# Attention in a hybrid decoder layer: the diagonal matrix of negated row maxima moves from one VectorE product to eight scaled ScalarE copies

## The chip, the cores and the metric

The kernel runs on one core of a Trainium2 chip, in one launch. The metric is device time in microseconds, the median of repeated runs; a profile of one more execution stands beside them. The engines are TensorE (PE in the rows), VectorE (DVE), ScalarE (ACT), GpSimd (POOL) and SyncE (SP), which issues the DMA transfers. Each engine works through its own list of instructions in order and meets the others through semaphores.

## The reference, cut to what matters

One decoder layer over 2048 positions with model width 1024. The part that matters here is the pair of attentions, each with 8 query heads of width 64: a sparse one (A) over selected keys, and a sliding-window one (B) over 128 keys with a learned sink per head.

```
# B, for each block of 128 queries
logits = q @ k.T * scale + bias;  masked to the window
m = max(max(logits, axis=-1), sink)
e = exp(logits - m)
p = e / (sum(e) + exp(sink - m))
o = p @ v
# A is a plain softmax over the selected keys: exp(logits - max) / sum, then @ v
```

So both need a row maximum per query and head, and both subtract it before the exponential.

## The kernel before, in words

The kernel has four stages one after the other: `front` (input projection, scores and selection), `attend`, `merge` (gates, output projection, layer norm) and `ffn`. The change is in `attend`, which takes about 775 to 1655 us of the profiled span.

`attend` works on 32 blocks b = 0 to 31: for each of the 16 tiles of 128 queries first kind 0 (attention A, with n+1 key tiles), then kind 1 (attention B, with two key tiles). Block b is `(kind, n) = (b % 2, b // 2)`. The logits are formed twice. The first time (`top`) they are laid out with queries on the partitions, in the two PSUM halves `sq`, and VectorE takes their maxima: kind 0 with the fused add and maximum on L951 into `mx`, kind 1 with a reduction on L940 into `mm8`. Then `negmax` finishes `mm8` [128 queries x 8 heads] (L960 for kind 0, L958 for kind 1) and builds `dg`, 128 x 1024: for each head the 128 x 128 matrix with the negated maximum on its diagonal, as the product of `nid` (the negated identity) and `mm8` on L963 (the statement begins on L963 and ends on L966). TensorE multiplies ones by `dg` (`spread`, L1141, two halves) and so has the negated maxima along the free axis in every row; ScalarE copies them into `q2` (L897), from where they come into the second set of logits as part of a matmul. In that second set (`logits`, L1097 to L1103, PSUM tile `stp`) keys are on the partitions. ScalarE takes the exponential (L868) and its rounded copy `phi` (L870), GpSimd the remainder `plo` (L810), and TensorE multiplies both with the values (`values`, L1122 to L1124) into `ov`. ScalarE and VectorE each empty half of `ov` after the last pair of a block (`finish`, L879 and L880 on ScalarE, L976 and L977 on VectorE).

The order on every engine comes from one list `plan`, made by a small planner in ticks: a tick has one `logits`, one `values` in two halves three steps behind, and in between up to five pieces of the next blocks' preparation (`q`, `kv`, `vt`, `top`, `max`, `spread`). Each engine walks the same list and does its own part of each entry. On ScalarE, `q` is two copies of the loaded queries (L842, L843), which VectorE then completes on L984; `kv` is two copies (L850, L851); `vt` two (L858, L859); `logits` is L868 and L870. Before the change, ScalarE does nothing at `max`, and goes past it. `max` stands right before the next block's `q` in most blocks, or before a `finish`, and `spread` comes one tick later.

These waits matter here. TensorE's `spread` waits for `dgd`, the finished `dg`. Its `logits` of a block wait for `q2d`, both halves of `q2`; a `top` that reuses a half of `sq` waits until what was in it is read; the first `values` of a block wait for `eva` and `evd`, the emptied `ov` of the block before.

Of the kernel before, what the change touches and what calls it, by code (L numbers as in the profile page):

```python
# [20 lines left out]
ALU = mybir.AluOpType  # L21
ACT = mybir.ActivationFunctionType
AX = mybir.AxisListType
# [5 lines left out]
P = 128  # L29
# [3 lines left out]
HEADS = 8  # L33
# [12 lines left out]
CH = 512  # L46
# [527 lines left out]
def stage_attend(nc, zt, mask, bands, sinks, yt, ident):  # L574

    with Stage(nc, "att") as s:
# [26 lines left out]
        nid = s.sb("nid", [P, P], F32)  # L603
        irep = s.sb("irep", [P, CH], BF16)
        ones = s.sb("ones", [P, P], F32R)
        dg = s.sb("dg", [P, QW], F32R)
# [3 lines left out]
        mx = s.sb("mx", [P, HEADS, NCH], F32)  # L610
        mm8 = s.sb("mm8", [P, HEADS], F32)
        snk = s.sb("snk", [P, HEADS], F32)
        early = ExitStack()

        def initial(name, shape):
# [12 lines left out]
        stp = s.ps("stp", [P, 2, QW])  # L628
        ov = s.ps("ov", [P, QW])
        banks = stp[:].rearrange("p a b -> p (a b)")  # L630
        names = ("lka", "lva", "lba", "lbq", "lsn", "rnd", "kdone", "tp", "tpe", "vdone", "bhd", "bld", "bqd", "c0", "c1", "c2", "cst",
                 "lq0", "lq1", "lm0", "lm1", "lm2", "lb0", "lb1", "qr", "qd", "kh", "kd", "vt", "vh", "vd", "sqd", "sqr", "dvl",
                 "dgd", "nm", "q2d", "std", "ex", "ph", "pl", "pv", "eva", "evd", "rc", "yd", "st0", "st1")
        S = {n: s.sem(n) for n in names}
# [16 lines left out]
        while nv < len(steps):  # L651
            room, left = [], 2.2
            while pend and left > 0.3 and len(room) < 5:
                op, b, x = pend[0]
# [34 lines left out]
            if go:  # L689
                b, i = steps[nv]  # L690
# [126 lines left out]
        @block.scalar  # L817
        def _(act):
            def round_bias(kind):
                act.wait_ge(S["lbq"], 16 * (kind + 1))  # L820
                act.activation(bq[:, kind], bqa[:], ACT.Copy).then_inc(S["bqd"], 1)

            def round_near(kind):
                act.wait_ge(S["lba"], 32 * (kind + 1))
                if kind:
                    act.wait_ge(S["rnd"], 2)
                act.activation(bhi[:, kind], ba[:], ACT.Copy).then_inc(S["bhd"], 1)

            act.wait_ge(S["lka"], 32)
            act.activation(khh[:], ka[:], ACT.Copy).then_inc(S["rnd"], 1)  # L830
            round_bias(0)
            for t in range(2):
                act.wait_ge(S["tp"], t + 1)
                act.activation(vhi[:, 8 * t:8 * t + 8, 0:DH], banks[:, t * CH:(t + 1) * CH].rearrange("p (n c) -> p n c", n=8),
                               ACT.Copy).then_inc(S["tpe"], 1)
            round_near(0)

            def queries(b):
                act.wait_ge(S[f"lq{b % 2}"], 32 * (b // 2 + 1))
                if b >= NQ:  # L840
                    act.wait_ge(S["std"], first[b - NQ + 1])
                act.activation(qst[:, b % NQ, :], kr[:, b % 2, :], ACT.Copy, scale=SCALE).then_inc(S["qr"], 1)  # L842
                act.activation(q2[0:DH, b % NQ, :], kr[0:DH, b % 2, :], ACT.Copy, scale=SCALE).then_inc(S["qr"], 1)  # L843

            def window_keys(n):
                act.wait_ge(S[f"lb{n % 2}"], 96 * (n // 2 + 1))
                act.wait_ge(S["c0"], 3)
                if n >= 2:
                    act.wait_ge(S["std"], first[index[1, n - 2] + 1])
                act.activation(khb[:, n % 2], kbr[:, n % 2, 0], ACT.Copy)  # L850
                act.activation(khb[:, 2 + n % 3], kbr[:, n % 2, 1], ACT.Copy).then_inc(S["kh"], 1)  # L851

            def window_values(n):
                act.wait_ge(S["vt"], n + 1)
                if n >= 2:
                    act.wait_ge(S["pv"], first[index[1, n - 2] + 1])
                src = sq[:, where[("vt", index[1, n], 0)] % 2, 0:2 * P].rearrange("p (v g d) -> p v g d", v=2, g=2)
                act.activation(vhb[:, n % 2, :, 0:DH], src[:, 0], ACT.Copy)  # L858
                act.activation(vhb[:, 2 + n % 3, :, 0:DH], src[:, 1], ACT.Copy).then_inc(S["vh"], 1)  # L859

            def exponential(k):
                act.wait_ge(S["std"], k + 1)
                if k == 0:
                    act.wait_ge(S["bld"], 2)
                    act.wait_ge(S["bqd"], 2)
                if k >= PS:
                    act.wait_ge(S["pv"], k - PS + 1)
                act.activation(pf[:, k % PS, :], stp[:, k % 2, :], ACT.Exp).then_inc(S["ex"], 1)  # L868
                act.wait_ge(S["ex"], k + 1)
                act.activation(phi[:, k % PS, :], pf[:, k % PS, :], ACT.Copy).then_inc(S["ph"], 1)  # L870

            def evict(b):
                act.wait_ge(S["pv"], first[b + 1])
                if b >= 2:
                    act.wait_ge(S[f"st{b % 2}"], 16 * (b // 2))
                oe = ov[:, 0:CH].rearrange("p (a e q) -> p a e q", a=2, e=2)
                for e in range(2):
                    rows = slice(e * DH, (e + 1) * DH)
                    act.activation(den[rows, b % 2, 0:2], oe[DH:P, :, e, :], ACT.Copy)  # L879
                    last = act.activation(y[rows, b % 2, 0:2], oe[0:DH, :, e, :], ACT.Copy)  # L880
                last.then_inc(S["eva"], 1)

            for op, b, x in plan:
                if op == "q":
                    queries(b)
                    if b == 1:
                        round_bias(1)
                        round_near(1)
                elif op == "kv":
                    window_keys(seq[b][1])  # L890
                elif op == "vt":
                    window_values(seq[b][1])
                elif op == "logits":
                    exponential(first[b] + x)
                elif op == "spread":
                    act.wait_ge(S["nm"], 2 * b + x + 1)
                    act.activation(q2[DH:P, b % NQ, x * CH:(x + 1) * CH], sq[DH:P, where[(op, b, x)] % 2, :], ACT.Copy).then_inc(S["q2d"], 1)  # L897
                elif op == "finish":
                    evict(b)

        @block.vector
        def _(dve):
            links = 0

            def link(ins):
                nonlocal links
                links += 1
                ins.then_inc(S["dvl"], 1)
                dve.wait_ge(S["dvl"], links)
# [22 lines left out]
            def top(b, x):  # L932
                kind, n = seq[b]
                h, c = x
                i = top_no[("top", b, x)]
                k = where[("top", b, x)] % 2
                dve.wait_ge(S["sqd"], i + 1)
                if kind:
                    w = P * min(2, n + 1)
                    dve.tensor_reduce(mm8[:, h:h + 2], sq[:, k, :].rearrange("p (a b) -> p a b", a=2)[:, :, 0:w],  # L940
                                      AX.X, ALU.max).then_inc(S["sqr"], 1)
                    return
                w = min(CH, (n + 1) * P - c * CH)
                if n >= 2:
                    dve.wait_ge(S[f"lm{n % 3}"], 16 * ((n - 2) // 3 + 1))
                    m = msk[:, n % 3, c * CH:c * CH + w]
                else:
                    m = cm[:, P - n * P:2 * P]
                if i >= 2:
                    dve.wait_ge(S["sqr"], i - 1)  # L950
                dve.tensor_tensor_reduce(junk[:, i % 2, 0:w], sq[:, k, 0:w], m, 1.0, 4 * NEG, ALU.add, ALU.max,  # L951
                                         mx[:, h, c:c + 1]).then_inc(S["sqr"], 1)

            def negmax(b):
                kind, n = seq[b]
                dve.wait_ge(S["sqr"], top_end[b])
                if kind:
                    link(dve.tensor_tensor(mm8[:], mm8[:], snk[:], ALU.max))  # L958
                else:
                    link(dve.tensor_reduce(mm8[:], mx[:, :, 0:-(-(n + 1) * P // CH)], AX.X, ALU.max))  # L960
                if b:
                    dve.wait_ge(S["nm"], 2 * b)
                dve.tensor_tensor(dg[:].rearrange("p (h q) -> p h q", h=HEADS),  # L963
                                  nid[:].rearrange("p (o q) -> p o q", o=1).broadcast_to([P, HEADS, P]),
                                  mm8[:].rearrange("p (h o) -> p h o", o=1).broadcast_to([P, HEADS, P]),
                                  ALU.mult).then_inc(S["dgd"], 1)  # L966
                dve.wait_ge(S["dgd"], b + 1)

            def evict(b):
                dve.wait_ge(S["pv"], first[b + 1])  # L970
                if b >= 2:
# [8 lines left out]
            for op, b, x in plan:  # L980
                kind, n = seq[b]
# [761 lines left out]
```

## Time and profile before

| | |
|---|---|
| median of 3 runs | 3795.15 us (3794.61 to 3798.49) |
| profiled execution | 3792.41 us, its span 3790.5 us |
| TensorE matmul busy | 3435.3 us (91%) |
| VectorE busy | 2545.7 us (67%) |
| ScalarE busy | 1647.2 us (43%) |
| GpSimd busy | 644.6 us (17%) |
| granted TensorE clock, mean | 0.956 of full speed |

Busy time is the union of an engine's instructions; waits, semaphores and the issuing of transfers are not in it. The shares are means over four stages, so they don't tell what limits `attend`. The span lacks 1.9 us of the execution's own time, which lie around it.

### The profile page before, as it was taken

How to read it: one execution, taken by the hardware profiler on the slowest of the kernel's cores; microseconds unless marked ns; L12 is line 12 of the kernel's file. 1: busy time of each engine (PE TensorE's matmuls, PEld its weight loads, DVE VectorE, ACT ScalarE, POOL GpSimd, SP SyncE). 2: the span in 40 equal slices, each digit the busy share in tenths (PEclk: the TensorE clock that was granted, in tenths of full speed). 3: DMA queues.
4: the chain of work that ended last, by engine and by line, in shares of the span. 5: the costliest groups of instructions: out<-in, count | busy, mean ns of one | idle time of the engine just before them, and what ended most of it. 6: DMA issues, size and time to landing. Idle time of an engine off the chain costs nothing. (4 is left out here: it accounts for less than half of the span.)

```text
span 3790.5 us, 40676 instructions
## 1 busy us (share of the span) xinstructions
PE 3435.3 (91%) x15064; PEld 2723.2 (72%) x15064; DVE 2545.7 (67%) x4109; ACT 1647.2 (43%) x2025; POOL 644.6 (17%) x367
## 2 busy tenths in 40 slices
PE   7999899947888899868888799999999999999997
PEld 5788677835556666646666688878888788878885
DVE  5899999957766675625555465557666766666565
ACT  5767777135566666652222133333333333333331
POOL 1022222324455556540000000000000000000000
PEclk9999999968899999989989899999999999999998
DMA  6323322342111111034344433223322332223220
GB/s 165 54 87 96 113 85 93 128 125 65 48 52 47 38 44 29 14 101 159 118 133 145 129 111 122 100 89 105 121 100 100 103 123 100 100 81 111 100 100 31
DMA packets 233023, 356.89 MB, mean 94 GB/s; under 512 B 43453, under 2 KB 150605, under 8 KB 218814
## 3 DMA queue, kind: packets, MB, share of 16 engines
q1 hardware_dynamic: 231774, 349.95, 29.8%
q0 software_dynamic: 1056, 4.36, 0.3%
q8 instruction: 122, 2.00, 0.2%
q14 instruction: 71, 0.58, 0.1%
HBM read 290.13 MB, written 64.13 MB: 93 GB/s over the span
## 5 line engine op out<-in xcount | busy, mean ns | idle before, releaser
L88 PE MATMUL ffn_up<-ffn_xh,ffn_uh 128*128 128x512 f32 x1536 | 599.2, 390 | 9.9 <-DVE ffn_ul L1519 9.9
L89 PE MATMUL ffn_up<-ffn_xl,ffn_uh 128*128 128x512 f32 x1536 | 598.7, 390 | 0.0
L90 PE MATMUL ffn_up<-ffn_xh,ffn_ul 128*128 128x512 f32 x1536 | 598.7, 390 | 0.0
L1477 ACT ACTIVATE ffn_c<-ffn_up,ffn_cb,ffn_cw 128x512 f32<-128x512 f32 x192 | 148.7, 777 | 766.5 <-PE ffn_up L90 760.8
L810 POOL TENSOR_TENSOR att_plo<-att_pf,att_phi 128x1024 fp32r<-128x1024 f32 x168 | 407.8, 2429 | 389.3 <-ACT att_phi L870 389.2
L88 PE MATMUL frt_acc<-frt_xh,frt_wh 128*128 128x512 f32 x864 | 339.5, 393 | 20.3 <-issue 9.6
L88 PEld LDWEIGHTS ffn_up<-ffn_xh,ffn_uh 128*128 128x128 f32 x1536 | 289.2, 188 | 70.7 <-DVE ffn_ul L1519 5.3
L90 PE MATMUL frt_acc<-frt_xh,frt_wl 128*128 128x512 f32 x864 | 337.9, 391 | 0.0
L89 PE MATMUL frt_acc<-frt_xl,frt_wh 128*128 128x512 f32 x864 | 337.7, 391 | 0.0
L90 PEld LDWEIGHTS ffn_up<-ffn_xh,ffn_ul 128*128 128x128 f32 x1536 | 289.0, 188 | 60.2
L89 PEld LDWEIGHTS ffn_up<-ffn_xl,ffn_uh 128*128 128x128 f32 x1536 | 289.2, 188 | 60.0
L1537 DVE COPY ffn_halo<-ffn_up 128x2 f32<-128x2 f32 x192 | 30.2, 157 | 442.0 <-ACT ffn_c L1477 441.8
L88 PE MATMUL ffn_dn<-ffn_dh,ffn_hh 128*128 128x512 f32 x768 | 303.3, 395 | 14.6 <-issue 14.6
L89 PE MATMUL ffn_dn<-ffn_dl,ffn_hh 128*128 128x512 f32 x768 | 301.9, 393 | 0.0
L90 PE MATMUL ffn_dn<-ffn_dh,ffn_hl 128*128 128x512 f32 x768 | 301.7, 393 | 0.0
L868 ACT ACTIVATE att_pf<-att_stp 128x1024 f32<-128x1024 f32 x168 | 172.1, 1024 | 274.3 <-PE att_stp L1100 155.7
L1611 POOL TENSOR_TENSOR ffn_rstd<-ffn_mv,ffn_mhalf 128x1 f32<-128x1 f32 x16 | 9.8, 611 | 1637.4 <-DVE ffn_mv L1570 1637.4
L951 DVE CUSTOM_DVE_ANT_0 att_junk<-att_sq,att_msk 128x512 bf16<-128x512 f32 (+3 forms) x304 | 183.2, 618 | 114.7 <-PE att_sq L1058 67.5
L1519 DVE TENSOR_TENSOR ffn_ul<-ffn_ur,ffn_uh 128x2048 fp32r<-128x2048 f32 x96 | 219.9, 2291 | 21.7 <-ACT ffn_uh L1459 21.7
L366 ACT ACTIVATE frt_junk<-frt_scb,frt_cand 128x1664 bf16<-128x1664 f32 (+1 forms) x124 | 226.6, 1828 | 0.0
L303 POOL TENSOR_TENSOR frt_wl<-frt_wr,frt_wh 128x1024 fp32r<-128x1024 f32 x51 | 125.3, 2461 | 495.2 <-ACT frt_wh L332 495.0
L88 PEld LDWEIGHTS frt_acc<-frt_xh,frt_wh 128*128 128x128 f32 x864 | 163.2, 189 | 58.2 <-issue 18.1
(268 smaller groups left out, 7518.4 us busy)
## 6 DMA issues: line engine op xcount, KB each, us to landing
ffn_ur<-in_w_up_dram SPq DMA_DIRECT2D x96, 1024.0 KB, 4.7
ffn_dr<-in_w_down_dram SPq DMA_DIRECT2D x64, 768.0 KB, 4.4
zt<-frt_out SPq DMA_DIRECT2D x108, 256.0 KB, 4.4
frt_wr<-in_w_main_dram SPq DMA_DIRECT2D x51, 512.0 KB, 4.2
att_raw<-zt SPq DMA_DIRECT2D x64, 256.0 KB, 4.1
mrg_gr<-zt SPq DMA_DIRECT2D x64, 256.0 KB, 4.2
frt_xr<-in_xt_dram SPq DMA_DIRECT2D x12, 1024.0 KB, 8.0
yt<-att_y SPq DMA_DIRECT2D x32, 256.0 KB, 2.3
```

Source lines behind the costliest of these rows:

```text
L88: pe.matmul(out, ahi, bhi, start=first, stop=False)
L89: pe.matmul(out, ahi, blo, start=False, stop=False)
L90: return pe.matmul(out, alo, bhi, start=False, stop=last)
L303: pool.tensor_tensor(wl[:, j % RW], wr[:, j % RW], f32(wh[:, j % RW]), ALU.subtract).then_inc(S["wld"], 1)
L366: act.activation(junk[:, counts % 2, 0:w], scores(i), ACT.Sign, scale=-1.0, bias=cand[:, i:i + 1].bitcast(F32), accum_out=cnt[:, i:i + 1]) ...
L810: pool.tensor_tensor(plo[:, k % PS, :], pf[:, k % PS, :], f32(phi[:, k % PS, :]), ALU.subtract).then_inc(S["pl"], 1)
L868: act.activation(pf[:, k % PS, :], stp[:, k % 2, :], ACT.Exp).then_inc(S["ex"], 1)
L951: dve.tensor_tensor_reduce(junk[:, i % 2, 0:w], sq[:, k, 0:w], m, 1.0, 4 * NEG, ALU.add, ALU.max, mx[:, h, c:c + 1]).then_inc(S["sqr"], 1)
L1477: act.activation(c[:, k % 2, a, :], up[:, k % 2, a, :], ACT.Identity, scale=cw[:, 2, a, k % NS:k % NS + 1], bias=cb[:, a, k % NS:k % NS + ...
L1519: dve.tensor_tensor(ul[:, k % 2], ur[:, k % 2], f32(uh[:, k % 2]), ALU.subtract).then_inc(S["uld"], 1)
L1537: dve.tensor_copy(halo[:, q % 2, a, t, :], src[:, TH - 2:TH])
L1611: pool.tensor_tensor(rstd[:, v % TB:v % TB + 1], mv[:, v % TB, 1:2], mhalf[:], ALU.pow).then_inc(S["pw"], 1)
```

## The change

`negmax` on VectorE ends with `mm8` and signals a new semaphore `pk`. At the `max` entry of the plan, ScalarE now waits for `pk` (and for `nm`, that the spread of the block before has read `dg`), and makes `dg` head by head: eight copies of the 128 x 128 negated identity, each scaled per partition by one column of `mm8`. The last one signals `dgd`. As `mm8` is now read by another engine, VectorE waits for `dgd` of the block before when it first writes `mm8` for a block.

```
-        names = ("lka", ...
+        names = ("pk", "lka", ...
...
+                elif op == "max":                       # ScalarE
+                    act.wait_ge(S["pk"], b + 1)
+                    act.wait_ge(S["cst"], 4)
+                    if b:
+                        act.wait_ge(S["nm"], 2 * b)
+                    for h in range(HEADS):
+                        last = act.activation(dg[:, h * P:(h + 1) * P], nid[:], ACT.Copy, scale=mm8[:, h:h + 1])
+                    last.then_inc(S["dgd"], 1)
...
                 if kind:                                # VectorE, top
                     w = P * min(2, n + 1)
+                    if b and h == 0:
+                        dve.wait_ge(S["dgd"], b)
...
                 if kind:                                # VectorE, negmax
-                    link(dve.tensor_tensor(mm8[:], mm8[:], snk[:], ALU.max))
+                    dve.tensor_tensor(mm8[:], mm8[:], snk[:], ALU.max).then_inc(S["pk"], 1)
                 else:
-                    link(dve.tensor_reduce(mm8[:], mx[:, :, 0:-(-(n + 1) * P // CH)], AX.X, ALU.max))
-                if b:
-                    dve.wait_ge(S["nm"], 2 * b)
-                dve.tensor_tensor(dg[:].rearrange("p (h q) -> p h q", h=HEADS),
-                                  nid[:].rearrange("p (o q) -> p o q", o=1).broadcast_to([P, HEADS, P]),
-                                  mm8[:].rearrange("p (h o) -> p h o", o=1).broadcast_to([P, HEADS, P]),
-                                  ALU.mult).then_inc(S["dgd"], 1)
-                dve.wait_ge(S["dgd"], b + 1)
+                    if b:
+                        dve.wait_ge(S["dgd"], b)
+                    dve.tensor_reduce(mm8[:], mx[:, :, 0:-(-(n + 1) * P // CH)], AX.X, ALU.max).then_inc(S["pk"], 1)
```

## Rows read from the trace of the kernel before

**Rows 1.** Waits, 770 to 1660 us: total us, times, longest us

```profile
PE att_sq L1141 <- DVE att_dg L963: 49.9, 27, 4.4
PE att_stp L1097 <- ACT att_q L897: 20.4, 10, 4.5
```

**Rows 2.** Windows: us, busy us by engine, granted clock, DMA share, GB/s

```profile
1207.00:1211.50 4.50, 4.47 (x18) 3.13 (x18) 0.00 (x0) 2.31 (x4) 1.38 (x2) 0.62 0.68 170
...
775.00:1610.00 835.00, 685.94 (x3090) 476.13 (x3090) 551.44 (x1118) 488.33 (x627) 428.11 (x202) 0.91 0.20 50
```

**Rows 3.** The tile `dg`: duration min/median/max, first and last start

```profile
L963 DVE TENSOR_TENSOR att_dg<-att_nid,att_mm x32: 1224/2070/3427, 818.1 to 1598.6; 128x1024 fp32r<-128x1024 f32 x32
```

**Rows 4.** VectorE's groups by form, 770 to 1660 us: busy, mean ns, idle before

```profile
L963 DVE TENSOR_TENSOR att_dg<-att_nid,att_mm 128x1024 fp32r<-128x1024 f32 x32 | 63.5, 1986 | 1.1
```

**Rows 5.** VectorE and GpSimd in order of time, block 3: start, us

```profile
869.47 3.27 DVE L963 TENSOR_TENSOR att_dg<-att_nid,att_mm 128x1024 fp32r<-128x1024 f32 x1
...
869.29 2.36 POOL L810 TENSOR_TENSOR att_plo<-att_pf,att_phi 128x1024 fp32r<-128x1024 f32 x1 [5.61 <-ACT att_phi L870]
```

**Rows 6.** ScalarE's groups by form: projections, then 1660 us to the end

```profile
L359 ACT ACTIVATE frt_out<-frt_acc 128x512 f32<-128x512 f32 x108 | 61.2, 585 | 74.3 <-PE frt_acc L90 74.3
...
L1477 ACT ACTIVATE ffn_c<-ffn_up,ffn_cb,ffn_cw 128x512 f32<-128x512 f32 x192 | 148.7, 777 | 766.5 <-PE ffn_up L90 760.8 <-DMA ffn_gb<-in_ln_b_dram 5.6
```

**Rows 7.** ScalarE in order of time around `max` of block 16

```profile
1149.25 1.06 ACT L870 ACTIVATE att_phi<-att_pf 128x1024 fp32r<-128x1024 f32 x1
...
1152.11 0.40 ACT L850 ACTIVATE att_khb<-att_kbr 128x256 fp32r<-128x256 f32 x1
1152.41 0.40 ACT L851 ACTIVATE att_khb<-att_kbr 128x256 fp32r<-128x256 f32 x1
1152.84 1.08 ACT L897 ACTIVATE att_q<-att_sq 64x512 fp32r<-64x512 f32 x2
...
1157.74 0.26 ACT L858 ACTIVATE att_vhb<-att_sq 128x128 fp32r<-128x128 f32 x1
1157.90 0.27 ACT L859 ACTIVATE att_vhb<-att_sq 128x128 fp32r<-128x128 f32 x1
```

**Rows 8.** VectorE and TensorE for block 16

```profile
1147.04 0.18 DVE L960 TENSOR_REDUCE att_mm<-att_mx 128x8 f32<-128x24 f32 x1
...
1154.06 0.47 PE L1097 MATMUL att_stp<-att_qst,att_khh 128*128 128x512 f32 x1 [2.13 <-ACT att_q L897]
```

**Rows 9.** Block 23: VectorE's last reduction, then ScalarE, then TensorE

```profile
1334.70 0.64 DVE L958 TENSOR_TENSOR att_mm<-att_mm,att_snk 128x8 f32<-128x8 f32 x1
...
1332.76 1.04 ACT L842 ACTIVATE att_qst<-att_raw 128x1024 fp32r<-128x1024 f32 x1
...
1335.00 1.02 ACT L868 ACTIVATE att_pf<-att_stp 128x1024 f32<-128x1024 f32 x1 [0.26 <-PE att_stp L1100]
...
1338.88 0.38 ACT L879 ACTIVATE att_den<-att_ov 64x256 f32<-64x256 f32 x1
...
1341.12 0.40 PE L1122 MATMUL att_ov<-att_phi,att_vhi 128*128 128x512 f32 x1
```

**Rows 10.** Block 31: VectorE, ScalarE, TensorE

```profile
1596.87 1.75 DVE L958 TENSOR_TENSOR att_mm<-att_mm,att_snk 128x8 f32<-128x8 f32 x1
...
1596.89 0.38 ACT L879 ACTIVATE att_den<-att_ov 64x256 f32<-64x256 f32 x1 [0.77 <-PE att_ov L1124]
...
1600.33 0.39 PE L1122 MATMUL att_ov<-att_phi,att_vhb 128*128 128x512 f32 x1
```

**Rows 11.** ScalarE after `max` of block 26

```profile
1436.95 1.03 ACT L868 ACTIVATE att_pf<-att_stp 128x1024 f32<-128x1024 f32 x1 [1.84 <-PE att_stp L1103]
```

**Rows 12.** ScalarE at the stage's start, around `max` of block 0

```profile
811.72 1.04 ACT L842 ACTIVATE att_qst<-att_raw 128x1024 fp32r<-128x1024 f32 x1
...
821.43 1.91 ACT L827 ACTIVATE att_bhi<-att_ba 128x2048 fp32r<-128x2048 f32 x1 [4.06 <-DVE att_ba L988]
...
823.98 1.08 ACT L897 ACTIVATE att_q<-att_sq 64x512 fp32r<-64x512 f32 x2
```

More of the change, by code:

```diff
@@ L630, in stage_attend @@
         banks = stp[:].rearrange("p a b -> p (a b)")
-        names = ("lka", "lva", "lba", "lbq", "lsn", "rnd", "kdone", "tp", "tpe", "vdone", "bhd", "bld", "bqd", "c0", "c1", "c2", "cst",
+        names = ("pk", "lka", "lva", "lba", "lbq", "lsn", "rnd", "kdone", "tp", "tpe", "vdone", "bhd", "bld", "bqd", "c0", "c1", "c2", "cst",
                  "lq0", "lq1", "lm0", "lm1", "lm2", "lb0", "lb1", "qr", "qd", "kh", "kd", "vt", "vh", "vd", "sqd", "sqr", "dvl",
```

## The prediction

> **What bounds the kernel now.** I read the page first: TensorE is busy 91% of the span, but that is a mean over four stages, and only `attend` is changed. The windows show that stage: of 835 us TensorE is busy 686, VectorE 551, ScalarE 488, GpSimd 428 [rows 2]. None is full. Then the waits: the longest that TensorE has in the stage, past its start, is on `dg`, 49.9 us in 27 waits, and the next on `q2`, which ScalarE copies, 20.4 us in 10 [rows 1]. So the chain from the last `top` through `mm8`, `dg`, `spread` and `q2` to the next logits does hold TensorE up; what counts is how long it gets, on whichever engine. Last, I laid the timeline of all four engines side by side around `max` in about a dozen of the 32 blocks, to see what ScalarE does there: it is hardly ever idle with nothing queued behind.
>
> **What goes.** 32 products on L963, 63.5 us of VectorE, 1.99 us each in the mean [rows 4], the shortest 1.22, the longest 3.43 [rows 3]. The long ones run beside GpSimd: in block 3 the product takes 3.27 us from 869.47, and GpSimd's L810 runs from 869.29 to 871.65, so the product ends 1.1 us after it [rows 5]. The link between reduction and product on VectorE costs almost nothing. A shared-port lock is what the Trainium skill (SBUF — State Buffer, Who interferes with whom) gives for this: an instruction of VectorE with two SBUF inputs and a reading one of GpSimd exclude each other, and ScalarE waits for nobody. The rows of block 3 agree. That speaks for the change, and by the rule alone every contended product would be freed of up to 2.2 us; the sum below has this in it already, as it goes by each block's own product.
>
> **What comes.** Eight copies of 128x128 from SBUF with a per-partition scale. No such row exists. Two copies of 128x256 from SBUF, back to back, start 0.30 us apart and take 0.40 each [rows 7]. ScalarE's 128x1024 copies take 1.06 [rows 7], so 768 elements are 0.66 us, and 128 fewer are 0.11: start to start 0.19. The scale comes from a tile, and the only group with such operands has two of them, scale and bias: 777 ns against 585 for the plain 128x512 copy [rows 6], so 0.09 to 0.10 for one. That gives 0.29 from start to start, 8 x 0.29 = 2.3 us of ScalarE's queue, and 2.4 until the last has ended. Bounds: below, the operand costs nothing and the copies go like those from PSUM, 0.16 apart [rows 7], 1.4 us in all; above, no overlap, 0.38 each, 3.0 us. I take 2.3, since both parts have a row of near kind. Total 74 us more on ScalarE for 64 less on VectorE.
>
> **The hand-off alone.** If one takes only when `dg` is ready (0.1 us from VectorE's end to ScalarE's start, 0.14 on to TensorE, and ScalarE not before its running copy ends) and compares block by block with when `spread` started, the 32 differences sum to +25 us at 2.4, and -7 at 1.4. In the late blocks, where the product ran alone in 1.22, it is +1.25 each; where it ran into GpSimd, -0.9.
>
> **What is queued behind.** ScalarE passed `max` without a wait. Now it stands there until VectorE's reduction, and behind it in its queue are the next block's `q`, the exponential of the next logits, the two `q2` copies, and an emptying of `ov`. TensorE waits for the last three. The blocks fall into five groups.
>
> *Eight even blocks, 2 and 12 to 24.* In block 16 the exponential's copy ends at 1150.31, long after `mm8` at 1147.22, and from there ScalarE runs without a pause to `q2` at 1152.84; TensorE had waited 2.13 us for that when it started logits at 1154.06 [rows 7, 8]. The copies push everything by their 2.3. 8 x 2.3 = 18.4.
>
> *Six odd blocks, 13 to 23.* Block 23: `mm8` is done at 1335.34 [rows 9]. ScalarE did `q` from 1332.76, the exponential from 1335.00, and emptied `ov` from 1338.88 to 1340.43 [rows 9]. Now: copies 1335.4 to 1337.7, `q` (2 x 0.95) to 1339.6, exponential pair (2.0) to 1341.7, two `q2` to 1342.7, `ov` (4 x 0.39) to 1344.3. The first `values` of the next block, at 1341.12 before [rows 9], start at 1344.4: +3.3. In the four earlier ones, with less slack lost, +3.0. Together 18.6. Most of this is not the copies but the wait: `q` used to run in ScalarE's free time.
>
> *Four late odd blocks, 25 to 31.* Block 31: `mm8` at 1598.62; the emptying that ran from 1596.89 now starts at 1601.0 and ends at 1602.6; `values` at 1600.33 move to 1602.7, +2.4 [rows 10]. Three like this, and block 25 at +1.2, where TensorE had waited for L984 anyway. 8.4.
>
> *Blocks 26, 28 and 30.* ScalarE waits 1.84 us for TensorE right behind `max` [rows 11], and the copies fit in that but for 0.5. 1.5.
>
> *Eleven early blocks, 0, 1 and 3 to 11.* In block 0 ScalarE did `q` of block 1 at 811.72, and `q2` at 823.98 [rows 12]; `mm8` comes at 818.1, so `q`, the two rounded bias tables (1.91 each [rows 12]) and `kv` follow from 820.5, and `q2` comes at 827: +3.0. Block 3 gains 0.9, as `dg` is ready at 871.9 instead of 872.74 [rows 5]. The others are between: 18.6 for the eleven.
>
> Sum 65.5. GpSimd and VectorE have more room, but TensorE waits for neither at these places, so nothing comes back. VectorE's new wait before it first writes `mm8` again costs nothing: `dg` of the block before is then several us old.
>
> **The clock.** Between 1207 and 1211.5 us, right after a wait of TensorE for `q2`, the granted clock is 0.62, partly at the lower of its two levels, 1.2 GHz, while TensorE is busy throughout; over the stage it is 0.91 [rows 2]. There are some two dozen such stretches in the stage, and each costs at most (1 - 0.62) x 4.5 = 1.7 us. More and longer waits make more of them; I put 6 us, 3 or 4 more that count. The Trainium skill (TensorE: Matmul & The Clock Gate, What's actually happening) says that the low level is the default and activity releases it. By it nearly every lengthened wait could bring a low stretch: that is the third rival.
>
> Sum 71.5. The profiled execution took 3792.4 us (span 3790.5 and 1.9 around it), so 3864; the median of the runs is 2.7 above it: 3866, rounded 3865.
>
> **Rivals.**
> *Only the hand-off counts.* ScalarE is busy 58% of the stage [rows 2], and may make up the queue's delay before TensorE asks. Then +25: 3820. Against it: blocks 16 and 23 show TensorE asking at once.
> *Faster.* The copies cost 1.4 us, and the backlog is hidden. Then -7 for the hand-off, and what VectorE's 64 us buy elsewhere, say 5 more: 3783. This decides only if the eight copies take under about 1.7 us, that is 0.2 each, and the wait at `max` holds nobody.
> *The clock.* Every block's longer wait brings a low stretch: 32 x 1.2 (part of it is under waits for ScalarE) in place of 6: +104, 3900.
> *No change.* The costs and gains of the hand-off cancel, at 0.2 us a copy: 3797.
>
> **How the numbers follow.** The forecast has 0.66, hand-off only 0.12, the clock 0.14, faster 0.04, no change 0.04. Its own range: copies from 1.4 to 3.0 us move the 25 or so blocks that pay by -0.9 to +0.7 each, -22 to +18, so 3843 to 3883; with part of the others, 3828 to 3900 leaves out about 2 in 10. Within 0.2% (7.6 us, about what a measurement of this kernel can tell from no change) 0.04, faster 0.04, slower 0.92.
>
> **What would show it.** After the change: the eight copies start 0.29 us apart (over 0.35 or under 0.2, and the sum moves by 18 or so); `q` in blocks 13 to 23 behind `max`, not before; TensorE's waits for `q2` (20 before) and for the emptied `ov` grow to some 60 us together, while those for `dg` rise by 10 to 25; the stage longer by about 70, the other stages unchanged; granted clock in the stage 0.87 to 0.90. It would be wrong if ScalarE's backlog from one `max` is gone before TensorE needs it, or if the copies overlap more than plain ones do.

## The result, and the profile after

The changed kernel takes 3854.61 us in the median (3853.27 to 3856.65, 4 runs) against 3795.38 of the kernel before: a ratio of 1.0155 with a 95% interval of 1.0137 to 1.0173, 59 us more. The forecast was 3865, with a range of 3828 to 3900. The page of the changed kernel begins so (busy us, share of the span, instructions):

```profile
span 3852.8 us, 40907 instructions
...
PE 3453.2 (90%) x15064; PEld 2736.0 (71%) x15064; DVE 2475.1 (64%) x4077; ACT 1721.8 (45%) x2281; POOL 631.8 (16%) x367
```

VectorE has 71 us less and ScalarE 75 us more. Where the time went shows in two windows: from the first `top` of `attend` to within 3 us of its last matmul, and from the last matmul to the end. The kernel before, columns as in [rows 2]:

```profile
813.00:1655.00 842.00, 727.25 (x3259) 505.21 (x3259) 537.58 (x1111) 509.05 (x651) 449.84 (x198) 0.93 0.17 43
...
1657.60:3790.50 2132.90, 1971.22 (x8576) 1619.96 (x8576) 1279.92 (x1915) 646.88 (x694) 21.12 (x34) 0.96 0.33 110
```

The changed kernel:

```profile
813.00:1711.00 898.00, 740.37 (x3257) 514.23 (x3258) 467.49 (x1079) 584.60 (x908) 437.34 (x198) 0.91 0.16 40
...
1714.00:3852.80 2138.80, 1974.83 (x8576) 1622.53 (x8576) 1279.55 (x1915) 647.05 (x694) 21.04 (x34) 0.96 0.33 110
```

The stage is 56 us longer. TensorE's matmuls, the same ones, take 13.1 us more of it (740.4 against 727.3, at a granted clock, the share of full speed that the chip allows, of 0.91 against 0.93), and TensorE is idle for 157.6 us (898.0 - 740.4) instead of 114.8: 42.9 more. The stages behind it are 5.9 us longer in this pair of executions, in code that is the same; the two profiled executions are 62 us apart (3854.8 and 3792.4) and the medians of the whole kernels 59, so some of that is the scatter between executions.

TensorE's waits in the changed kernel, 820 to 1715 us (total us, times, longest us), which answer to [rows 1]:

```profile
PE att_sq L1145 <- ACT att_dg L901: 77.8, 32, 3.6
PE att_stp L1101 <- ACT att_q L905: 23.1, 10, 6.4
PE att_sq L1055 <- DVE att_vlb L1003: 22.8, 13, 2.1
PE att_ov L1126 <- ACT att_y L880: 20.2, 17, 1.7
...
PE att_sq L1062 <- ACT att_q L905: 2.3, 2, 1.4
```

The wait for `dg` is there in all 32 blocks now, 77.8 us in place of 49.9, and the wait for the emptied `ov` (L880) has grown from 4.1 us in 3 blocks to 20.2 us in 17.

The copies themselves, on ScalarE, and VectorE's completion of `q` (by tile: duration min/median/max; by group, 770 to 1720 us):

```profile
L901 ACT ACTIVATE att_dg<-att_nid,att_mm x256: 384/386/403, 818.4 to 1653.1; 128x128 fp32r<-128x128 f32 x128
```

```profile
L901 ACT ACTIVATE att_dg<-att_nid,att_mm 128x128 fp32r<-128x128 f32 x256 | 78.1, 387 | 49.1 <-DVE att_mm L968 33.9 <-DVE att_mm L972 15.0
...
L988 DVE SCALAR_TENSOR_TENSOR att_qst<-att_raw,att_qst 64x1024 fp32r<-64x1024 f32 x32 | 40.0, 1248 | 134.4 <-ACT att_q L843 134.4
```

A copy takes 386 ns and never over 403, so none is stretched by GpSimd. ScalarE stands idle ahead of them for 49.1 us, waiting for `mm8`: time in which it did `q` or emptied `ov` before. VectorE waits 134.4 us for `q` instead of 42. The Trainium skill (ScalarE: Activation LUTs, What ACT_TABLE_LOAD costs) gives 186 ns plus 0.833 per element of the row for an activation and about 93 for each operand that is a pointer; for 128 elements and one pointer that is an estimate of 386 ns, and the row agrees.

Block 16 in the changed kernel, ScalarE and then TensorE, to set beside [rows 7] and [rows 8]:

```profile
1176.05 1.06 ACT L870 ACTIVATE att_phi<-att_pf 128x1024 fp32r<-128x1024 f32 x1
1177.01 2.43 ACT L901 ACTIVATE att_dg<-att_nid,att_mm 128x128 fp32r<-128x128 f32 x8
1179.35 1.04 ACT L842 ACTIVATE att_qst<-att_raw 128x1024 fp32r<-128x1024 f32 x1
...
1181.98 1.08 ACT L905 ACTIVATE att_q<-att_sq 64x512 fp32r<-64x512 f32 x2
...
1179.59 0.48 PE L1145 MATMUL att_sq<-att_dg,att_ones 128*128 128x512 f32 x1 [3.23 <-ACT att_dg L901]
1183.20 0.47 PE L1101 MATMUL att_stp<-att_qst,att_khh 128*128 128x512 f32 x1 [1.51 <-ACT att_q L905]
```

ScalarE's queue has no gap here: the exponential's copy, the eight copies (2.34 us from the start of the first to the start of `q`), `q`, `kv`, `q2`. From the start of L870 to that of `q2` it was 3.59 us before and is 5.93 now. TensorE's `spread` in the same block of the kernel before:

```profile
1149.82 0.47 PE L1141 MATMUL att_sq<-att_dg,att_ones 128*128 128x512 f32 x1 [0.27 <-DVE att_dg L963]
```

Its two waits in this block, for `dg` and for `q2`, were 0.27 and 2.13 us, and are 3.23 and 1.51: together 2.34 more, the length of the copies. The wait for `q2` itself is shorter, because more of the lateness is met at `dg`, which TensorE asks for first.

Block 23, of the kind for which the prediction put most on ScalarE's wait, to set beside [rows 9]; VectorE, ScalarE, then TensorE:

```profile
1380.10 0.63 DVE L968 TENSOR_TENSOR att_mm<-att_mm,att_snk 128x8 f32<-128x8 f32 x1
...
1377.18 1.06 ACT L870 ACTIVATE att_phi<-att_pf 128x1024 fp32r<-128x1024 f32 x1
1380.76 2.44 ACT L901 ACTIVATE att_dg<-att_nid,att_mm 128x128 fp32r<-128x128 f32 x8 [2.53 <-DVE att_mm L968]
1383.11 1.04 ACT L842 ACTIVATE att_qst<-att_raw 128x1024 fp32r<-128x1024 f32 x1
...
1385.01 1.00 ACT L868 ACTIVATE att_pf<-att_stp 128x1024 f32<-128x1024 f32 x1
...
1387.13 1.08 ACT L905 ACTIVATE att_q<-att_sq 64x512 fp32r<-64x512 f32 x2
1388.23 0.38 ACT L879 ACTIVATE att_den<-att_ov 64x256 f32<-64x256 f32 x1
...
1383.35 0.76 PE L1145 MATMUL att_sq<-att_dg,att_ones 128*128 128x512 f32 x1 [2.99 <-ACT att_dg L901]
1389.92 0.47 PE L1126 MATMUL att_ov<-att_phi,att_vhi 128*128 128x512 f32 x1 [1.45 <-ACT att_y L880]
```

ScalarE stands 2.53 us before the copies, with `q` behind it. `mm8` is ready at 1380.10 + 0.63 = 1380.73, and the first `values` of the next block start 9.2 us after it; in the kernel before it was 1341.12 - 1335.34 = 5.8. That is 3.4 later; the prediction had followed the queue to 3.3. And the first half of `spread` takes 0.76 us here, against 0.48 in block 16, with the granted clock partly at the lower of its two levels, 1.2 GHz. The window behind its start in the changed kernel:

```profile
1383.00:1387.00 4.00, 3.65 (x10) 2.85 (x10) 1.33 (x2) 3.97 (x5) 0.00 (x0) 0.57 0.00 0
```

### The profile page after: what moved, and what is told of

Same layout as the page of the kernel before. It is cut to its first block and busy times, and to the rows that moved or that the text cites. A ratio compares the mean times of both kernels' runs of the same rounds, so it can differ in the third digit from the quotient of the medians.

```text
span 3852.8 us, 40907 instructions
## 1 busy us (share of the span) xinstructions
PE 3453.2 (90%) x15064; PEld 2736.0 (71%) x15064; DVE 2475.1 (64%) x4077; ACT 1721.8 (45%) x2281; POOL 631.8 (16%) x367
```

## The experiments

All times are against the kernel before, and each difference is worked out from the ratio. (The lines of code are edits of the kernel before for e1, e2, e4, e5, e8 and the filling; for e3, e6 and e7 they are edits of the change.) The stage is the window from 813 us to within 3 us of its last matmul; "idle" is its length less TensorE's busy time, from the same row. (The rows of e1 to e4 lack some 50 of TensorE's 3259 matmul records each, so their busy time may be short by a few us; the others, filling aside, differ from 3259 by two at most. The profiled executions of e2 and e6 are the longest of their four: 3831.0 us at a median of 3826.2, and 3887.3 at 3874.1.)

| kernel | ratio, 95% | difference, us | stage | TensorE busy | idle | clock |
|---|---|---|---|---|---|---|
| before | | | 842 | 727.3 | 114.8 | 0.93 |
| the change | 1.0155 [1.0137, 1.0173] | +59 | 898 | 740.4 | 157.6 | 0.91 |
| e1, wait only | 0.9986 [0.9974, 0.9998] | -5 | 842 | 724.6 | 117.4 | 0.93 |
| e2, copies only | 1.0067 [1.0044, 1.0090] | +25 | 874 | 738.2 | 135.9 | 0.92 |
| e3, copies late | 1.0202 [1.0184, 1.0220] | +77 | 922 | 750.8 | 171.2 | 0.88 |
| e4, halves on VectorE | 0.9997 [0.9987, 1.0008] | -1 | 848 | 731.5 | 116.5 | 0.93 |
| e5, wait and copies | 1.0204 [1.0188, 1.0219] | +77 | 921 | 760.1 | 160.9 | 0.89 |
| e6, early signal | 1.0208 [1.0180, 1.0236] | +79 | 930 | 770.5 | 159.5 | 0.88 |
| e7, shared | 1.0066 [1.0049, 1.0083] | +25 | 870 | 736.5 | 133.5 | 0.92 |
| e8, eight on VectorE | 1.0021 [1.0011, 1.0031] | +8 | 852 | 734.5 | 117.5 | 0.92 |
| e9, before + 3 filling | 0.9993 [0.9984, 1.0003] | -3 | 844 | 746.0 | 98.0 | 0.94 |
| e10, before + 6 filling | 0.9983 [0.9974, 0.9993] | -6 | 839 | 751.4 | 87.6 | 0.97 |
| e11, early signal + 6 filling | 1.0204 [1.0187, 1.0221] | +77 | 920 | 791.3 | 128.7 | 0.91 |
| e12, the change + 6 filling | 1.0154 [1.0137, 1.0172] | +58 | 904 | 773.8 | 130.2 | 0.93 |

Theory 1, the queue: the loss comes from what stands behind `max` in ScalarE's queue. Theory 2, the hand-off: it comes from `dg` being ready later.

**e1, the wait alone.** The product stays on VectorE.

```
+                elif op == "max":                       # ScalarE
+                    act.wait_ge(S["pk"], b + 1)
...
-                    link(dve.tensor_tensor(mm8[:], mm8[:], snk[:], ALU.max))
+                    dve.tensor_tensor(mm8[:], mm8[:], snk[:], ALU.max).then_inc(S["pk"], 1)
...
+                dve.wait_ge(S["pk"], b + 1)
```

> The kernel before, in which ScalarE only waits at `max` for the finished `mm8`, and VectorE still makes `dg`. No copies. Queue theory (what stands behind `max` on ScalarE is late, by the wait and by the copies): the wait alone costs where ScalarE used the time for `q` or for emptying `ov`; by block 23's rows `q` starts at 1335.4 instead of 1332.8, and the first `values` move by 1.0; in the late odd blocks 0; in all about +10 us (5 to 20) against the kernel before. Rival, the hand-off alone costs (the copies are longer than the product): nothing is handed to ScalarE here, so 0.

-5 us (-10 to -1 by the interval). The +10 of the queue theory was wrong, and its range of 5 to 20 too: alone, the wait costs nothing. (`pk` also replaces the link between VectorE's two instructions here.)

**e2, the copies alone**, beside the product, without the wait.

```
+        spare = s.sb("spare", [P, QW], BF16)
...
+                elif op == "max":                       # ScalarE
+                    act.wait_ge(S["cst"], 4)
+                    act.wait_ge(S["lsn"], 16)
+                    for h in range(HEADS):
+                        act.activation(spare[:, h * P:(h + 1) * P], nid[:], ACT.Copy, scale=snk[:, h:h + 1])
```

> The kernel before, with eight scaled copies of 128x128 at `max` on ScalarE into a tile that nobody reads (bf16, scaled by the sinks), without the wait for `mm8`; VectorE still makes `dg`. Queue theory: the eight even blocks pay 2.3 each as with the change, the odd ones 13 to 23 about 0.6 each, the rest little: about +26 us (18 to 36). Rival, the hand-off alone: the copies are in nobody's chain, 0. Wait and copies together then make less than the change, since its odd blocks pay for both in a row.

+25 us, as the queue theory had it. TensorE's waits, 820 to 1690 us:

```profile
PE att_sq L1147 <- DVE att_dg L969: 50.7, 27, 4.4
PE att_stp L1103 <- ACT att_q L903: 39.0, 13, 5.2
```

The wait for `dg` is as before [rows 1], and the one for `q2` has nearly doubled, from 20.4 to 39.0.

**e3, the copies later in ScalarE's queue.**

```
+            def diagonal(b):
+                act.wait_ge(S["pk"], b + 1)
...
+                for h in range(HEADS):
+                    last = act.activation(dg[:, h * P:(h + 1) * P], nid[:], ACT.Copy, scale=mm8[:, h:h + 1])
+                last.then_inc(S["dgd"], 1)
...
             for op, b, x in plan:
+                if owed and op in ("logits", "spread"):
+                    diagonal(owed.pop())
...
                 elif op == "max":
-                    act.wait_ge(S["pk"], b + 1)
...
+                    owed.append(b)
```

> The changed kernel, with the eight copies later in ScalarE's queue: behind the `q`, `kv` and `finish` that follow `max`, right before the next `logits` or `spread`. Same work, same wait, same hand-off. Queue theory: in the odd blocks `q` and the emptying of `ov` run before the wait again: +1.4 instead of +3 in blocks 13 to 23, +1.2 in the late ones, the even ones as before at 2.3; about +40 us over the kernel before (30 to 50), so some 20 under the change. Rival, the hand-off alone: `dg` comes no sooner than with the change, so as the change, +59 or more.

+77, where I had said +40 and the rival +59. Both missed. ScalarE in this kernel around block 6, early in the stage:

```profile
939.81 0.38 ACT L879 ACTIVATE att_den<-att_ov 64x256 f32<-64x256 f32 x1 [2.47 <-PE att_ov L1134]
...
941.38 1.06 ACT L842 ACTIVATE att_qst<-att_raw 128x1024 fp32r<-128x1024 f32 x1
...
943.90 2.43 ACT L889 ACTIVATE att_dg<-att_nid,att_mm 128x128 fp32r<-128x128 f32 x8
947.28 0.59 ACT L911 ACTIVATE att_q<-att_sq 64x512 fp32r<-64x512 f32 x1 [0.95 <-PE att_sq L1151]
948.98 0.59 ACT L911 ACTIVATE att_q<-att_sq 64x512 fp32r<-64x512 f32 x1 [1.11 <-PE att_sq L1151]
```

`mm8` was done at 940.0. The emptying, `q` and `kv` now stand ahead of the copies (4.1 us), and after the copies ScalarE has nothing to do but to wait for `spread`, where `q` had filled that gap. I had counted what the copies no longer hold up, and not what holds up the copies. TensorE's wait for `dg` is 129.7 us in this kernel. So a late `dg` does cost, when it is 4 us late.

**e5, wait and copies together, nothing handed off.** e2 with `pk` as in e1: ScalarE's queue is that of the change, while VectorE makes the `dg` that is used.

```
                 elif op == "max":
+                    act.wait_ge(S["pk"], b + 1)
                     act.wait_ge(S["cst"], 4)
```

> The kernel before, with ScalarE's queue as in the change: at `max` it waits for `mm8` and then makes eight scaled copies (bf16, scaled by the sinks, into a tile that nobody reads), while VectorE makes the `dg` that TensorE uses. The wait alone had cost nothing and the copies alone 26 us, of the change's 59. Queue theory: the two in a row do what neither does alone, since the copies can no longer lie in the time before `mm8`; `q2` and the emptied `ov` come as late as with the change: +50 us (42 to 60). Rival, the remaining 33 us are the hand-off (`dg` itself is later, as ScalarE starts it late and takes 2.4 us): this kernel hands nothing off, so the parts add up to +26 (20 to 32).

+77, far from the rival's 26 and above the queue theory's 50 (42 to 60) as well. The parts, -5 and +25, don't add up; in a row they make more than three times their sum. TensorE's waits, 820 to 1715 us, then the stage:

```profile
PE att_sq L1149 <- DVE att_dg L971: 47.8, 26, 4.4
PE att_stp L1105 <- ACT att_q L904: 47.4, 14, 7.7
PE att_ov L1130 <- ACT att_y L881: 24.8, 19, 2.3
```

```profile
813.00:1734.00 921.00, 760.13 (x3258) 528.47 (x3259) 527.48 (x1111) 584.72 (x908) 441.49 (x198) 0.89 0.16 39
```

`dg` is awaited no longer than before the change, and yet TensorE is idle for 160.9 us, about as long as with the change (157.6). The 28 us of waits that the change put on `dg` stand elsewhere here: compared with the change, the wait for `q2` is 24 us longer and that for `ov` 5. Block 16 shows it, `spread` and then the `logits`:

```profile
1189.83 0.47 PE L1149 MATMUL att_sq<-att_dg,att_ones 128*128 128x512 f32 x1 [0.27 <-DVE att_dg L971]
...
1196.40 0.77 PE L1105 MATMUL att_stp<-att_qst,att_khh 128*128 128x512 f32 x1 [4.48 <-ACT att_q L904]
```

The wait for `dg` is the 0.27 us of the kernel before, and that for `q2` 4.48: together 4.75, against 4.74 with the change. This is the main result: the idle time needs no hand-off. (VectorE still makes its products here and is busy 527 us of the stage, against 467 with the change. What that is worth by itself was not tested.)

**e6, the early signal.** The change, with each half of `spread` waiting for its own four copies.

```
                         last = act.activation(dg[:, h * P:(h + 1) * P], nid[:], ACT.Copy, scale=mm8[:, h:h + 1])
-                    last.then_inc(S["dgd"], 1)
+                        if h % 4 == 3:
+                            last.then_inc(S["dgd"], 1)
...
-                    pe.wait_ge(S["dgd"], b + 1)
+                    pe.wait_ge(S["dgd"], 2 * b + x + 1)
```

> The changed kernel, with a signal after the fourth copy too, and each half of `spread` waiting for its own half of `dg`. ScalarE's queue is the same to the instruction; only `spread` can start 1.15 us sooner. Hand-off theory: `dg` sooner by 1.15 in 32 blocks, -37 us at most, so some +25 to +35 over the kernel before. Queue theory: TensorE then waits for the emptied `ov` and for `q2`, which come no sooner: +50 (45 to 57).

+79. TensorE's waits, 820 to 1715 us, and the stage:

```profile
PE att_sq L1146 <- ACT att_dg L901: 46.1, 31, 2.7
PE att_stp L1102 <- ACT att_q L906: 40.2, 15, 6.8
PE att_ov L1127 <- ACT att_y L880: 31.0, 17, 2.3
```

```profile
813.00:1743.00 930.00, 770.51 (x3260) 530.23 (x3261) 474.24 (x1080) 584.60 (x909) 437.19 (x198) 0.88 0.15 39
```

The wait for `dg` falls by 32 us, nearly the 37 that the hand-off theory had at most, and all of it comes back: 17 us on `q2`, 11 on `ov` and 7 on `top`s that wait for a half of `sq`. TensorE is idle for 159.5 us against 157.6. So the hand-off is not what limits the change. But both theories had this kernel no slower than the change, and it is 20 us slower, in matmuls that take longer: 770.5 against 740.4 us, at 0.88 instead of 0.91. (Part of the 770.5 belongs to this execution, 13 us over the median; but over the whole kernel the granted clock is 0.942 to 0.946 in all four executions of e6, and 0.949 to 0.952 in those of the change.) e5 has slower matmuls too, 760.1. The last four kernels test what such slow matmuls cost.

**e7, shared.** Four copies on ScalarE, the product of the other four heads on VectorE at the same time.

```
-                    for h in range(HEADS):
+                    for h in range(4):                  # ScalarE, then dgd
...
+                dve.tensor_tensor(dg[:, CH:QW].rearrange("p (h q) -> p h q", h=4),
...
+                                  ALU.mult).then_inc(S["dgv"], 1)
...
+                    pe.wait_ge(S["dgv" if x else "dgd"], b + 1)
```

> The changed kernel, with ScalarE making four copies (heads 0 to 3) and VectorE at the same time the product for heads 4 to 7; each half of `spread` waits for its maker. Both theories: less than the change, as the copies in ScalarE's queue are 1.15 us in place of 2.3 and the first half of `dg` is ready sooner. Queue theory: half of what the copies cost beyond the wait, so +28 (20 to 36). Hand-off theory: `dg` is ready 1.25 us behind `mm8` as in the kernel before where the product ran alone, and sooner where it ran into GpSimd: 0 to +12.

+25, near the queue theory's 28 and outside the hand-off theory's 0 to +12. Half the copies cost less than half of the change's loss.

**e4, the product in halves on VectorE.**

```
+                for x in range(2):
+                    hs = slice(4 * x, 4 * x + 4)
+                    dve.tensor_tensor(dg[:, x * CH:(x + 1) * CH].rearrange("p (h q) -> p h q", h=4),
...
+                                      mm8[:, hs].rearrange("p (h o) -> p h o", o=1).broadcast_to([P, 4, P]),
+                                      ALU.mult).then_inc(S["dgd"], 1)
...
+                    pe.wait_ge(S["dgd"], 2 * b + x + 1)
```

> The kernel before, with VectorE's product in two halves of four heads, each with its own signal, and each half of `spread` waiting for its own. A version for this chain's latency. Theory that the chain behind `mm8` holds TensorE up at most blocks: the first half is ready some 0.6 us sooner where the product runs alone, and the second is covered by the `values` half between the two spreads: -12 us (-6 to -18). If TensorE's wait for `dg` were given back at its next wait for `q2` or `ov`, it would be 0 to -3.

-1, where -12 was expected: what was gained is given back. The wait for `dg` fell from 49.9 to 38.3 us, and idle is 116.5 against 114.8, though ScalarE's queue is unchanged.

**e8, eight products on VectorE**, with the maximum as a per-partition scalar, signalled in two halves.

```
+                for h in range(HEADS):
+                    last = dve.tensor_scalar(dg[:, h * P:(h + 1) * P], nid[:], mm8[:, h:h + 1], None, ALU.mult)
+                    if h % 4 == 3:
+                        last.then_inc(S["dgd"], 1)
```

> The kernel before, with VectorE making `dg` in eight products of 128x128 with the per-partition maximum as the scalar operand, signalled in two halves. One tile operand in place of two. If it is the second operand from SBUF that makes the product collide with GpSimd's L810, no copy here is stretched: eight at about 0.2 us, 1.6 in all, the first half after 0.8: -5 to -20 us. If they collide all the same, or a small product costs 0.3, it is 0 to +15.

+8. Duration min/median/max:

```profile
L964 DVE TENSOR_SCALAR att_dg<-att_nid,att_mm x256: 270/279/2520, 818.2 to 1608.4; 128x128 fp32r<-128x128 f32 x128
```

Small products cost 279 ns, and one tile operand doesn't keep them apart from GpSimd: the longest takes 2.52 us, and all 24 of the 256 that take over 1 us overlap an instruction of GpSimd. The Trainium skill (SBUF — State Buffer, Who interferes with whom) names `tensor_scalar` among those that can take the port pair shared with GpSimd, in a two-port mode; the stretched products agree with that, though no row here shows the mode itself.

**e9 to e12, filling matmuls.** Matmuls of constants into the half of `sq` that `spread` is about to overwrite, ahead of the wait for `dg`: three (e9) or six (e10) in the kernel before, six in e6 (e11) and six in the change (e12). The lines show six.

```
                     r = bank((op, b, x))
+                    for _ in range(6 if x == 0 else 0):
+                        pe.matmul(sq[:, r, :], idb[:], irep[:], start=True, stop=True)
                     pe.wait_ge(S["dgd"], b + 1)
```

> The kernel before, with three more matmuls (bf16 constants, 128x512) on TensorE into the free half of `sq` right ahead of its wait for `dg`, overwritten by `spread`. It leaves nothing out and adds work that fits in the wait of some 1.8 us. Clock theory (idle TensorE time brings stretches at the low clock, and they cost what the waits themselves don't): fewer such stretches, -5 to -15 us. If the clock doesn't hang on these waits: 0 to +3.

> The same with six filling matmuls, 1.4 us at the high clock, 2.6 at the low one. Clock theory: -8 to -20 us, unless they run over the wait at the low clock or in the even blocks in which there is hardly a wait, which costs up to 10. If the clock doesn't hang on these waits: +5 to +15.

> The changed kernel with the early signal after the fourth copy, which was 79 us over the kernel before while TensorE was idle no longer than with the change itself, now with six filling matmuls ahead of the wait for `dg`. Clock theory: the 20 us by which the early signal is worse than the change are time at the low clock, and the filler gives most of them back and some of the change's own: +50 (40 to 60) over the kernel before. If they are something else, +79 or more.

> The change, with the same six filling matmuls. Its waits for `dg` are 2.4 us in the mean, so the filler fits. Clock theory: the part of the change's loss that is TensorE running slower (13 us) goes: +42 (32 to 50) over the kernel before. Otherwise as the change, +59.

-3, -6, +77 and +58. The clock theory had -5 to -15, -8 to -20, +50 and +42: it was right about the clock and wrong about the time. The stage in e10, and its filling matmuls:

```profile
813.00:1652.00 839.00, 751.40 (x3450) 509.50 (x3451) 542.74 (x1111) 509.50 (x652) 449.78 (x198) 0.97 0.17 43
```

```profile
L1141 PE MATMUL att_sq<-att_irep,att_idb 128*128 128x512 bf16 x192 | 49.1, 394 | 0.1
```

The same in e11:

```profile
813.00:1733.00 920.00, 791.27 (x3450) 535.14 (x3451) 469.60 (x1080) 584.61 (x908) 437.49 (x198) 0.91 0.16 40
```

```profile
L1146 PE MATMUL att_sq<-att_irep,att_idb 128*128 128x512 bf16 x192 | 49.4, 395 | 0.1
```

In e10 the kernel's own matmuls take 751.4 - 49.1 = 702.3 us, 25 less than in the kernel before, and the clock rises from 0.93 to 0.97. But filling and idle together are 136.7 us in place of 114.8, 22 more. In e11 it is 741.9, 29 less than in e6 (some of it because e6's execution was a long one), and 178.1 for filling and idle, 19 more; its waits for `q2` and `ov` stay:

```profile
PE att_stp L1102 <- ACT att_q L906: 41.9, 15, 7.1
PE att_ov L1127 <- ACT att_y L880: 34.1, 21, 2.3
```

e12 is the same again: 724.7 for its own, 16 less than in the change, and 22 more of filling and idle. TensorE runs faster and waits longer. e10 may beat the kernel before, by 0.17% (0.07 to 0.26), and so may e1, by 0.14% (0.02 to 0.26); both are below the 0.2% that was set as the least difference that tells.

## Why the prediction was right

**The copies' price** was right to the row: 386 ns, eight in 2.44 us, 0.29 from start to start, where 0.29 and 2.4 had been worked out.

**The queue.** The start of VectorE's last reduction in each block, after less before, gives how much each block adds. By the prediction's groups, from its 32 starts and the stage's end in each trace. The forecast is of waits alone, so TensorE's idle time is what answers to it; the other part is matmuls that take longer or shorter (rounding leaves 0.1):

| blocks | forecast | measured | of it idle | of it matmuls |
|---|---|---|---|---|
| eight even, 2 and 12 to 24 | 18.4 | 18.4 | 13.4 | 5.1 |
| six odd, 13 to 23 | 18.6 | 16.8 | 10.2 | 6.6 |
| four late odd, 25 to 31 | 8.4 | 8.0 | 3.0 | 5.1 |
| 26, 28, 30 | 1.5 | -1.4 | -0.4 | -1.0 |
| eleven early | 18.6 | 14.3 | 16.5 | -2.2 |
| together | 65.5 | 56.1 | 42.7 | 13.5 |

So the full agreement of the even blocks is partly luck: of their 18.4, 5.1 is not waiting. In block 31 too, the emptying of `ov` ran right behind the copies, and the `values` waited for it:

```profile
1651.01 2.44 ACT L901 ACTIVATE att_dg<-att_nid,att_mm 128x128 fp32r<-128x128 f32 x8 [2.52 <-DVE att_mm L968]
1653.48 0.38 ACT L879 ACTIVATE att_den<-att_ov 64x256 f32<-64x256 f32 x1
...
1655.17 0.76 PE L1126 MATMUL att_ov<-att_phi,att_vhb 128*128 128x512 f32 x1 [0.80 <-ACT att_y L880]
```

**The sizes.** The agreement of the sum is partly luck between two terms. The prediction had 65.5 us of waits and 6 of slower matmuls. The stage has 42.9 and 13.1. The terms' sum, 71.5, was 12 over the measured 59.

The term "what is queued behind" was too large by some 23 us, 19 of it in the even, odd and late odd blocks. A delay that was followed to one wait of a block was taken as lasting, and part of it is made up later: in block 23 the `values` are 3.4 us later, as forecast, but by the next block's last reduction 2.05 are left, 1.24 of them idle time. In block 16 all of it lasts: 2.34.

The clock's term was too small by half. In the trace's record of the granted clock, the stage of the kernel before has 23 stretches at the low level, 115 us together, and TensorE is busy in 99 of them; the change has 27 stretches, 157 us, busy in 127. The number grew as forecast, by 4, but so did the mean length, from 5.0 to 5.8 us. At half the clock, 99 and 127 us of matmuls are 50 and 63 us more than at the full one. So a stretch cost 2.2 us in the mean even before the change, where the prediction had 1.7 at most, and the 14 us between 50 and 63 (unrounded) make up the 13.1 measured.

**The signs.** The copies 0.29 us apart and `q` behind them were as forecast. The waits were split otherwise: those for `q2` and `ov` are 43 us together and not 60, and that for `dg` rose by 28, not by 10 to 25. Read alone, that would speak for the hand-off; block 16 and e5 show the same lateness of ScalarE's queue, met one wait earlier. The stage grew by 56 us, not 70, and the clock of 0.91 is just above the 0.87 to 0.90.

**What was said of the causes.** "Most of this is not the copies but the wait", of the odd blocks, isn't borne out as put: e1 shows the wait alone to cost nothing. Wait and copies together do (e5). A reading that fits, but that no run tests by itself: the wait takes the time in which the copies could have hidden, and the copies the time in which the wait could have been made up for.

**The rivals.** Only the hand-off, +25: e5 has no hand-off and is idle as long as the change, and e6 hands off sooner and gains nothing. Faster, and no change: both needed copies of 0.2 us or less, and a backlog that holds nobody; neither is so. The clock at +104: the clock fell to 0.91 only. The rows show that work in the waits raised the clock (e10, 0.93 to 0.97); the Trainium skill's sentence that activity releases it (TensorE: Matmul & The Clock Gate, What's actually happening) agrees. What it was worth is another matter: 6 us in e10, 1 and 2 in e12 and e11.

**What stays open.** Why e5 and e6 have 20 and 30 us of slower matmuls more than the change, at the same idle time. It is the clock: their stages have 211 and 220 us at the low level, with TensorE busy in 169 and 181 of them, which by the same working are 35 and 41 us more than in the kernel before, where 33 and 43 were measured. But their waits are split differently, and which pattern of waits lowers the clock wasn't settled. That the slow matmuls cause the 20 us in time is not shown either: in e11 29 us of them went away, and the median fell by 2.

## What to carry to other kernels

Before work is moved to an engine that is free on average, follow that engine's queue from the point where the work goes in: a wait for another engine's result there, followed by 2.4 us of copies, held up three things that the engine which sets the pace needed (`dg`, `q2` and the emptied `ov`), and cost 59 us for 64 us taken off VectorE. Test the wait and the work both apart and together: apart they cost -5 and +25 us, together +77. And when one wait of that engine shrinks and its others grow by as much (e4, e6), the time is set by something else, in e6 by ScalarE's queue, and a signal given sooner did not help. The wait that has grown in the profile (`dg`, by 28 us) need not name the cause: it is only the first that meets the lateness.

## What the runs showed of the hardware that I hadn't expected

`tensor_scalar` of 128x128 in fp32 on VectorE, with one tile operand, is stretched beside GpSimd like the product with two: 279 ns in the median, 2520 at most, and all 24 of 256 that take over 1 us overlap an instruction of GpSimd (e8). Six filling matmuls a block raised the granted clock of the stage from 0.93 to 0.97 and made the kernel's other matmuls 25 us shorter in sum, for a gain of 6 us (e10).
